# Two expert layers on one Trainium2 core: the result rows of each expert are scattered to their token's place by rank of the choice, and summed from plain loads

## The chip, the cores and the metric

The kernel runs on one core of one Trainium2 chip. The metric is the device time of one execution in microseconds (us). Engines are named as in the profile: PE (TensorE matmuls), PEld (its weight loads), DVE (VectorE), ACT (ScalarE), POOL (GpSimd) and SP (SyncE, which here only issues transfers). "ACTq", "SPq" and "POOLq" are an engine's own queue of such issuing instructions.

## The reference

Two layers of a diffusion backbone over 512 tokens of width 1,024. Each layer ends in a mixture of 16 experts. The router picks one group of four experts for a token and two experts inside it:

```python
def moe_route(flat, router_w, router_b):
    s = jax.nn.sigmoid((flat @ router_w).astype(jnp.float32))
    biased = s + router_b.astype(jnp.float32)
    grp_score = jnp.sum(lax.top_k(biased.reshape(n, 4, 4), 2)[0], axis=-1)
    g_sel = jnp.argmax(grp_score, axis=-1)
    in_group = (jnp.arange(16) // 4)[None, :] == g_sel[:, None]
    _, idx = lax.top_k(jnp.where(in_group, biased, -jnp.inf), 2)
    w = jnp.take_along_axis(s, idx, axis=-1)
    w = w / jnp.sum(w, axis=-1, keepdims=True)

for e in range(16):
    hid = jax.nn.silu(flat @ w_gate[e]) * (flat @ w_up[e])      # 1024 -> 512
    out = out + combine[:, e:e + 1] * (hid @ w_down[e])         # 512 -> 1024
```

So 512 tokens give 1,024 result rows of 4 KB, 64 to an expert on average. What a token receives is the weighted sum of two such rows.

## The kernel before

The kernel is written engine by engine, with semaphores counted. The two layers' expert parts (`moe(0, block)` and `moe(1, block)`) differ only in their data and in what follows them.

**Lists.** At the start of an expert part DVE turns the scores into the two chosen experts of each token and their places in the experts' lists. PE multiplies one-hot matrices of the places with the token numbers (L2106) and so writes, for each expert, a list of up to 128 token numbers. An expert with fewer tokens has empty places, which hold token 0. Were an expert chosen by more than 128 tokens, a second, slow branch (`If(most > P)`) would take the rest; in the traced execution no engine enters it.

**Steps.** One step handles one expert, and the order inside it is written by hand. POOL fetches the expert's 128 rows with one indirect DMA from `xh_scratch` (`fetch`, L1827) four steps ahead. PE transposes them (L2113). All matmuls are made of high and low parts: ACT casts each weight half to its high part (`high`, L1855), DVE subtracts it from the weights to get the low part (`low`, L2011), and PE multiplies 24 times 512 columns for gate, up and down each (L2130, L2145). SP loads the weights in halves of 1 MB into three ring slots. DVE multiplies the result by a gate into `y_sb` (`rows_out`, L2035; two halves at L2077 for the last expert). PE's step e waits with its last third for `rows_out` of expert e-1. `y_sb` has two buffers: `rows_out(e)` waits for the store of expert e-2.

**Stores.** ACT stores the 128 rows of an expert to the expert's own 128 rows of `y_scratch` (`store`).

**Tail.** After the last store has landed (`moe_stored`), POOL fetches with eight indirect DMAs (4 tiles of 128 tokens, 2 choices each; `Combine.fetch`, L2379) each token's two result rows by the row numbers `row_of`. DVE adds each to the residual `x` with its weight (`Combine.add`, L2394). Behind it:

- in layer 0: squares, norm and pooling of layer 1's mixer on ACT, POOL and PE, weights multiplied by a gate on DVE (`p_wg`, L2486 and L2488), the loads of the next router's rows on SP (`front1.load_rows`, L258 to L260, which overwrite the raw pooling weights and so wait for `p_wg`), and `front1.scales` (L324), which stands on DVE ahead of its part of the pooled columns (L2497);
- in layer 1: the final norm (L2574 on ACT, L221 and L223 on POOL, L2591 on DVE) and the stores of the output.

`rows_out` with its two waits:

```python
def rows_out(n, u, down_used, stored):
    dve.wait_ge(s_used, down_used)
    dve.wait_ge(s_yst[u], stored)
    V.tensor_tensor(y_sb[:, u, :], bank[:, 6:8, :], gate2_b[:], ALU.mult).then_inc(s_y, 1)
```

Of the kernel before, what the change touches and what calls it, by code (L numbers as in the profile page):

```python
# [49 lines left out]
LIST_N = NE * SEQ  # L50
# [15 lines left out]
def constants():  # L66
# [34 lines left out]
    token = np.arange(SEQ, dtype=np.int32).reshape(NT, P).T  # L101
# [9 lines left out]
def build_program(nc, a, out):  # L111
    ctx = ExitStack()
    with ctx, nc.allow_non_contiguous_dma(reason="short rows of small tables"):
# [21 lines left out]
        list_dram = nc.dram_tensor("list_scratch", [SEQ // P - 1, P, NE], I32).ap()  # L135
        y_dram = nc.dram_tensor("y_scratch", [LIST_N, D], F32).ap()
# [29 lines left out]
        row_of = sb("row_of", [P, 2, NT], U32)  # L166
# [1517 lines left out]
        def moe(l, block):  # L1684
# [50 lines left out]
            listed, at_small[0] = carve(at_small[0], 2 * NT * NE // 2)  # L1735
# [3 lines left out]
            row_tmp = small_tile("row_tmp", [P, 2, 2, NT])  # L1739
# [3 lines left out]
            lists_more = small_tile("lists_more", [P, SEQ // P - 1, NE], I32)  # L1743
            idx = small_tile("idx", [P, 1], U32)
# [17 lines left out]
            s_yst = [e_(f"y_stored{u}") for u in range(2)]  # L1762
# [7 lines left out]
            FIRST_BANK, LIST_BANK = 4, 3  # L1770
# [54 lines left out]
            def _(pool):  # L1825
                def fetch(u, rows):
                    pool.indirect_dma_start(out=xg[:, u, :], out_offset=None, in_=xh_dram,  # L1827
                                            in_offset=bass.IndirectOffsetOnAxis(ap=rows, axis=0)
                                            ).then_inc(s_xg[u], 16)
# [4 lines left out]
                fetch(0, idx[:])  # L1834
                nc.gpsimd.memset(mark[:], 0.0).then_inc(s_first_rows, 1)  # L1835
                pool.wait_ge(s_lists, 1)
                for m in range(1, NE):
                    u = m % 2
                    if m >= 2:
                        pool.wait_ge(s_gt, m - 1)  # L1840
                        pool.wait_ge(s_xg[u], 16 * (m // 2))
                    fetch(u, lists[:, m:m + 1])
# [4 lines left out]
            def _(act):  # L1847
# [25 lines left out]
                def store(e, u):  # L1873
                    act.wait_ge(s_y, e + 1)
                    act.dma_start(y_dram[bass.ds(e * P, P), :], y_sb[:, u, :]).then_inc(s_yst[u], 16)

                def step(e, u):
# [15 lines left out]
                    if not (isinstance(e, int) and e == 0):  # L1893
                        store(e - 1, 1 - u)
# [14 lines left out]
                store(LAST - 1, 0)  # L1909
                for hf in range(2):  # L1910
                    act.wait_ge(s_y, LAST + 1 + hf)
                    cols_ = slice(hf * HALF, (hf + 1) * HALF)
                    act.dma_start(y_dram[LAST * P:NE * P, cols_], y_sb[:, 1, cols_]).then_inc(s_yst[1], 16)
                for u in range(2):
# [700 lines left out]
```

## Time and profile before

| | us |
|---|---|
| median of 3 runs | 1114.15 (1113.95 to 1116.16) |
| the profiled execution's own time | 1112.38 |
| its span, first to last instruction | 1110.7 |
| busy: PE, DVE, ACT, POOL | 989.0, 939.0, 626.4, 104.4 |
| expert part of layer 0, up to its last result rows | 418.9 to 720.6 |
| tail of layer 0 and layer 1's mixer and router | 720.6 to 778.1 |
| expert part of layer 1, up to its last result rows | 778.1 to 1080.2 |
| tail of layer 1 | 1080.2 to 1110.7 |

The busy times are sums over the whole span; the span less an engine's busy time is its idle time. The last four lines come from the timeline. The traffic of the whole execution was 332.41 MB at a mean of 299 GB/s.

### The profile page before, as it was taken

To read this page: it belongs to the slowest core of one execution; us is meant where nothing else is said; L and a number is where in the kernel's file an instruction comes from. 1 tells how busy PE (TensorE), PEld (TensorE's weight loads), DVE (VectorE), ACT (ScalarE), POOL (GpSimd) and SP (SyncE) were. 2 spreads that over 40 slices of the span, in tenths; PEclk is the share of its full clock that TensorE was granted. 3 is DMA by queue.
4 is the path that set the end of the run, shared out by engine and by line. 5 is a ranking of instruction groups with operands and counts; after the bars stand their busy time and mean duration, and the time that the engine had idled before them with its cause. 6 is when DMAs were issued, how large, how long until landed. Compare 5 with 4: busy or idle time off the path is not lost. (4 is left out here: it accounts for less than half of the span.)

```text
span 1110.7 us, 14060 instructions
## 1 busy us (share of the span) xinstructions
PE 989.0 (89%) x4898; PEld 802.4 (72%) x4898; DVE 939.0 (85%) x1045; ACT 626.4 (56%) x770; POOL 104.4 (9%) x132
## 2 busy tenths in 40 slices
PE   6689999999798986999999999948799999999980
PEld 1467877777676865788888888737578888888870
DVE  5768988998797858899999999865899999999975
ACT  1635233324676135777777777443477777777741
POOL 0200120000110002000000000042300000000005
PEclk9989999999999998999999999969799999999995
DMA  9726878942301836999999999876599999999946
GB/s 368 286 75 211 280 244 308 323 172 96 151 1 53 309 113 237 345 413 414 415 413 415 413 414 412 296 259 263 205 353 413 413 415 413 414 413 414 414 169 236
DMA packets 148263, 332.41 MB, mean 299 GB/s; under 512 B 16444, under 2 KB 18404, under 8 KB 148088
## 3 DMA queue, kind: packets, MB, share of 16 engines
q1 hardware_dynamic: 127592, 278.72, 65.5%
q10 hardware_dynamic: 13712, 27.92, 7.2%
q0 software_dynamic: 6912, 25.17, 6.0%
q8 instruction: 27, 0.44, 0.2%
q14 instruction: 20, 0.16, 0.0%
HBM read 308.67 MB, written 23.11 MB: 299 GB/s over the span
## 5 line engine op out<-in xcount | busy, mean ns | idle before, releaser
L1855 ACT CAST w_hi<-ring 128x2048 fp32r<-128x2048 f32 x192 | 367.1, 1916 | 112.2 <-PE bank L2130 55.1
L2011 DVE TENSOR_TENSOR w_lo<-ring,w_hi 128x2048 fp32r<-128x2048 f32 x192 | 428.8, 2284 | 1.4 <-POOL mark L1835 1.0
L2130 PE MATMUL bank<-w_hi,xT_hi 128*128 128x512 f32 x512 | 203.4, 397 | 5.2 <-DVE xT_lo L2018 5.2
L2130 PE MATMUL bank<-w_hi,xT_lo 128*128 128x512 f32 x512 | 200.0, 391 | 0.0
L2130 PE MATMUL bank<-w_lo,xT_hi 128*128 128x512 f32 x512 | 199.5, 390 | 0.0
L1511 PE MATMUL bank<-ring_last_parts,arena_parts 128*128 128x512 f32 (+1 forms) x320 | 117.5, 398 | 8.0 <-DVE x_parts L1073 6.5
L2130 PEld LDWEIGHTS bank<-w_hi,xT_hi 128*128 128x128 f32 x512 | 96.1, 188 | 26.1 <-DVE xT_lo L2018 6.9
L2130 PEld LDWEIGHTS bank<-w_hi,xT_lo 128*128 128x128 f32 x512 | 96.2, 188 | 20.8
L2130 PEld LDWEIGHTS bank<-w_lo,xT_hi 128*128 128x128 f32 x512 | 96.3, 188 | 19.1
L1511 PE MATMUL bank<-ring_parts,arena_parts 128*128 128x512 f32 (+1 forms) x256 | 101.0, 395 | 0.0
L1145 DVE SCALAR_TENSOR_TENSOR gate_b<-ring,silu_c,gate_b 128x512 f32<-128x512 f32 x126 | 95.5, 758 | 4.5
L2145 PE MATMUL bank<-w_hi,hT_hi 128*128 128x512 f32 x240 | 93.6, 390 | 0.0
L2145 PE MATMUL bank<-w_lo,hT_hi 128*128 128x512 f32 x240 | 93.5, 389 | 0.0
L2145 PE MATMUL bank<-w_hi,hT_lo 128*128 128x512 f32 x240 | 93.4, 389 | 0.0
L1827 POOL DMA_INDIRECT shared<-xh_scratch,shared x32 | 37.5, 1171 | 428.1 <-PE bank L2113 406.3
L1511 PE MATMUL bank<-ring_last_parts,x_parts 128*128 128x512 f32 x192 | 77.7, 405 | 0.0
L1511 PEld LDWEIGHTS bank<-ring_last_parts,arena_parts 128*128 128x128 f32 x320 | 61.1, 194 | 20.9 <-DVE x_parts L1073 5.8
L1511 PEld LDWEIGHTS bank<-ring_parts,arena_parts 128*128 128x128 f32 x256 | 49.4, 193 | 8.8
L2145 PEld LDWEIGHTS bank<-w_hi,hT_hi 128*128 128x128 f32 x240 | 45.1, 188 | 9.3
L2145 PEld LDWEIGHTS bank<-w_hi,hT_lo 128*128 128x128 f32 x240 | 45.0, 188 | 9.4
L2145 PEld LDWEIGHTS bank<-w_lo,hT_hi 128*128 128x128 f32 x240 | 45.1, 188 | 9.3
L869 ACT ACTIVATE ada_junk<-bank 128x128 f32<-128x128 f32 x80 | 21.0, 278 | 48.0 <-PE bank L1481 25.2
(273 smaller groups left out, 1427.8 us busy)
## 6 DMA issues: line engine op xcount, KB each, us to landing
ring<-in_moe_w_gate SPq DMA_DIRECT2D x64, 1024.0 KB, 9.1
ring<-in_moe_w_down SPq DMA_DIRECT2D x64, 1024.0 KB, 9.6
ring<-in_moe_w_up SPq DMA_DIRECT2D x64, 1024.0 KB, 11.8
ring<-in_ada_w SPq DMA_DIRECT2D x18, 2048.0 KB, 9.1
y_scratch<-shared ACTq DMA_DIRECT2D x30, 512.0 KB, 6.2
ring<-in_w_in ACTq DMA_DIRECT2D x21, 512.0 KB, 4.6
shared<-in_ada_w SPq DMA_DIRECT2D x6, 1024.0 KB, 13.3
x_res<-in_x SPq DMA_DIRECT2D x8, 512.0 KB, 12.1
```

The lines of the kernel that those rows point to most:

```text
L869: last = nc.scalar.activation(ada_junk[:, c * P:(c + 1) * P], bank[:, 7 if i < IN_PROJ else 6 + i - IN_PROJ, c * P:(c + 1) * P], ACT.Ident ...
L1145: ins = nc.vector.scalar_tensor_tensor(ada_acc[:, i % 2, :], w[:, k, :], silu_c[:, 0, k:k + 1], onto, ALU.mult, ALU.add)
L1511: last = pe.matmul(acc(u)[:, c0:c1], hs[h_], ws[w_], start=(kk == 0 and i == 0), stop=(kk == KD - 1 and i == 2))
L1827: pool.indirect_dma_start(out=xg[:, u, :], out_offset=None, in_=xh_dram, in_offset=bass.IndirectOffsetOnAxis(ap=rows, axis=0)).then_inc(s_ ...
L1855: nc.scalar.copy(w_hi[:, buf(u, p), :], half(raw(e, p))).then_inc(s_hi, 3 if isinstance(e, int) and (e, p) == (-1, 3) else 1)
L2011: V.tensor_tensor(w_lo[:, buf(u, p), :], half(raw(e, p)), w_hi[:, buf(u, p), :].bitcast(F32), ALU.subtract).then_inc(s_lo, 3 if isinstance ...
L2130: last = pe.matmul(bank[:, b, :], xs[:, kk, :], ws[:, k, :], start=(kk == 0 and i == 0), stop=(kk == KD - 1 and i == 2))
L2145: last = pe.matmul(bank[:, 6 + hf, :], xs[:, kk, :], ws[:, k, at], start=(kk == 0 and i == 0), stop=(kk == KE - 1 and i == 2))
```

## The change

- Each list entry gets a second number, the destination: the token's number, plus 512 if this expert is the token's choice with the higher expert number ("rank 1"). `y_scratch` shrinks to 2 x 512 rows: rank 0 of all tokens, then rank 1. Eight more matmuls on PE make the destination lists (`dests`), DVE gets a few small operations for them.
- Lists hold the number minus 1,024, and 1,024 is added as they are copied, so that an empty place holds 1,024. The fetches get a bounds check and skip such places; the stale row in `xg` is multiplied and its result is dropped.
- ACT's plain stores go. POOL scatters `y_sb` by an indirect DMA with a bounds check (`scatter`), each behind a fetch in POOL's program.
- The weights of a token's two choices are put in order of rank.
- The tail's eight indirect fetches go. SP issues eight plain loads of 512 KB into ring slots 2 and 1 (`Combine.load`): four of rank 0 once all experts but the last are scattered, four of rank 1 once the last is. DVE adds all of rank 0 first. In layer 0 the gated pooling weights are made in two parts between the adds, and `front1.load_rows` waits for both; in layer 1 the load of the final norm's weights moves behind the eight loads.

```diff
-            def fetch(self, pool, most, moe_stored):
-                def tiles(written):
-                    for t in range(NT):
-                        for c in range(2):
-                            pool.indirect_dma_start(
-                                out=self.rows[:, c, t, :], out_offset=None, in_=y_dram[0:written, :],
-                                in_offset=bass.IndirectOffsetOnAxis(ap=row_of[:, c, t:t + 1], axis=0)
-                            ).then_inc(self.loaded[c][t], 16)
...
+            def load(self, sp, y_scattered):
+                for c in range(2):
+                    y_scattered(sp, NE - 1 + c)
                     for t in range(NT):
+                        at = (c * NT + t) * P
+                        sp.dma_start(self.rows[c][:, t, :], y_dram[at:at + P, :]).then_inc(self.loaded[c][t], 16)
...
+            def y_scattered(eng, experts):
+                for u in range(2):
+                    eng.wait_ge(s_yst[u], 16 * ((experts + 1 - u) // 2))
...
                 def fetch(u, rows):
                     pool.indirect_dma_start(out=xg[:, u, :], out_offset=None, in_=xh_dram,
-                                            in_offset=bass.IndirectOffsetOnAxis(ap=rows, axis=0)
+                                            in_offset=bass.IndirectOffsetOnAxis(ap=rows, axis=0),
+                                            bounds_check=SEQ - 1, oob_is_err=False
                                             ).then_inc(s_xg[u], 16)
...
+                def scatter(e):
+                    pool.wait_ge(s_y, NE + 1 if e == LAST else e + 1)
+                    if e == 0:
+                        pool.wait_ge(s_dests, 1)
+                    pool.indirect_dma_start(out=y_dram,
+                                            out_offset=bass.IndirectOffsetOnAxis(ap=dests[:, e:e + 1], axis=0),
+                                            in_=y_sb[:, e % 2, :], in_offset=None, bounds_check=2 * SEQ - 1,
+                                            oob_is_err=False).then_inc(s_yst[e % 2], 16)
+
-                for m in range(1, NE):
+                for m in range(1, NE + 5):
                     u = m % 2
+                    if m < NE:
                         if m >= 2:
                             pool.wait_ge(s_gt, m - 1)
                             pool.wait_ge(s_xg[u], 16 * (m // 2))
                         fetch(u, lists[:, m:m + 1])
+                    if m >= 5:
+                        scatter(m - 5)
...
-                def store(e, u):
-                    act.wait_ge(s_y, e + 1)
-                    act.dma_start(y_dram[bass.ds(e * P, P), :], y_sb[:, u, :]).then_inc(s_yst[u], 16)
...
+                    for c in range(2):
+                        ins = V.tensor_tensor(later[:, c], e_sel[:, c], e_sel[:, 1 - c], ALU.is_gt)
+                    link(ins)
+                    link(V.scalar_tensor_tensor(dest[:], later[:], float(SEQ),
+                                                token_f[:].unsqueeze(1).to_broadcast([P, 2, NT]), ALU.mult, ALU.add))
+                    for c in range(2):
+                        ins = V.tensor_tensor(listed[:, c, :, NE:2 * NE], pick[:, c], cols(dest[:, c], NE), ALU.mult)
+                    ins.then_inc(s_dest, 1)
...
                 rows_T(1, 16)
+                pe.wait_ge(s_dest, 1)
+                for c in range(2):
+                    for t in range(NT):
+                        last = pe.matmul(bank[:, DEST_BANK, DEST_AT:DEST_AT + NE], slot_of[:, c, t, :],
+                                         listed[:, c, t, NE:2 * NE], start=(c == 0 and t == 0), stop=(c == 1 and t == NT - 1))
+                last.then_inc(s_in_dests, 1)
                 product(3, -1, 0, 2, 0)
...
@@ layer 0, SP and DVE behind the expert part
-                sp.wait_ge(p_wg, 1)
+                combine.load(sp, y_scattered)
+                sp.wait_ge(p_wg, 2)
                 sp.wait_ge(combine.done, NT - 1)
                 front1.load_rows(sp)
...
+                for t in range(NT):
+                    combine.add(dve, 0, t)
                 dve.wait_ge(tables, 16 * 8)
...
+                gated_weights(0)
                 for t in range(NT):
-                    combine.add(dve, t)
+                    combine.add(dve, 1, t)
+                gated_weights(1)
                 front1.scales(dve)
...
@@ layer 1, SP and DVE behind the expert part
                 y_ready(sp)
+                combine.load(sp, y_scattered)
                 sp.dma_start(fin_w, a["final_norm_w"].partition_broadcast(P)).then_inc(f_ld, 16)
...
-                combine.add(dve, 0)
-                combine.add(dve, 1)
+                for t in range(NT):
+                    combine.add(dve, 0, t)
+                combine.add(dve, 1, 0)
+                combine.add(dve, 1, 1)
                 dve.wait_ge(f_ld, 16)
                 for t in range(NT):
                     if t + 2 < NT:
-                        combine.add(dve, t + 2)
+                        combine.add(dve, 1, t + 2)
                     dve.wait_ge(f_rs, t + 1)
```

How POOL's program reads at the start of an expert part, before (a row is a line, an operation and its tiles; `shared` holds `xg` and `y_sb`):

```order
L1831 CAST shared<-shared 128x128
L1832 MEMSET shared 128x128
L1827 DMA shared<-xh_scratch,shared 128x1024
L1835 MEMSET mark 1x1
L1827 DMA shared<-xh_scratch,shared 128x1024 x15
L1844 TENSOR_LOAD max_count
```

And after the change, the same place:

```order
L1837 CAST shared<-shared 128x128
L1838 MEMSET shared 128x128
L1832 DMA shared<-xh_scratch,shared 128x1024
L1841 MEMSET mark 1x1
L1832 DMA shared<-xh_scratch,shared 128x1024 x5
L1849 DMA y_scratch<-shared 1024x1024
L1832 DMA shared<-xh_scratch,shared 128x1024
L1849 DMA y_scratch<-shared 1024x1024
```

From the sixth fetch on, each is followed by the scatter of the expert five places earlier; after the last fetch the scatters of experts 11 to 15 stand in a row, ahead of the load of `max_count`.

DVE's program behind layer 0's expert part, before:

```order
L2484 SCALAR_TENSOR_TENSOR mod<-mod 128x8
L2485 TENSOR_SCALAR mod<-mod 128x8
L2486 TENSOR_TENSOR gate_b<-gate_b,shared 128x1024
L2488 TENSOR_TENSOR arena<-shared,gate_b 128x4x256 x2
L2394 SCALAR_TENSOR_TENSOR x_res<-arena,weight,x_res 128x1024 x8
L324 SCALAR_TENSOR_TENSOR shared<-shared,arena 128x1024
L2497 TENSOR_SCALAR arena<-bank,mod 128x512 x4
```

And after:

```order
L2428 SCALAR_TENSOR_TENSOR x_res<-ring,weight,x_res 128x1024 x4
L2517 SCALAR_TENSOR_TENSOR mod<-mod 128x8
L2518 TENSOR_SCALAR mod<-mod 128x8
L2519 TENSOR_TENSOR gate_b<-gate_b,shared 128x1024
L2521 TENSOR_TENSOR arena<-shared,gate_b 128x4x256
L2428 SCALAR_TENSOR_TENSOR x_res<-ring,weight,x_res 128x1024 x4
L2521 TENSOR_TENSOR arena<-shared,gate_b 128x4x256
L323 SCALAR_TENSOR_TENSOR shared<-shared,arena 128x1024
L2533 TENSOR_SCALAR arena<-bank,mod 128x512 x4
```

The gate and half of the gated weights have moved from before the adds to between the two ranks' adds, the other half behind them.

SP's program at the end of layer 1, before:

```order
L2228 REGISTER_ALU
L2228 COMPARE_AND_BRANCH
L2243 UNCONDITIONAL_BRANCH
L2564 DMA shared<-in_final_norm_w 128x1024
L2567 DMA out<-shared 128x1024 x4
L2548 UNCONDITIONAL_BRANCH
```

And after:

```order
L2255 COMPARE_AND_BRANCH
L2270 UNCONDITIONAL_BRANCH
L2420 DMA ring<-y_scratch 128x1024 x8
L2600 DMA shared<-in_final_norm_w 128x1024
L2603 DMA out<-shared 128x1024 x4
L2584 UNCONDITIONAL_BRANCH
```

The eight loads now stand ahead of the final norm's weights in SP's queue.

## Rows read from the trace of the kernel before

**Rows 1.** The profile page, its first line.

```profile
span 1110.7 us, 14060 instructions
```

**Rows 2.** Busy times in one step: PE, PEld, DVE, ACT, POOL; clock, DMA share, GB/s.

```profile
857.70:875.40 17.70, 17.70 (x86) 14.78 (x85) 16.78 (x11) 13.31 (x10) 0.94 (x1) 1.00 1.04 414
```

**Rows 3.** Waits from 850 to 1040 us: total, times, longest; DVE's only row.

```profile
DVE hT_lo L2028 <- ACT hT_hi L1871: 10.2, 11, 0.9
```

**Rows 4.** Timeline, POOL and DVE in two steps: start, us, what, [idle before].

```profile
851.52 0.94 POOL L1827 DMA_INDIRECT shared<-xh_scratch,shared  x1 [16.75 <-PE bank L2113]
869.20 0.94 POOL L1827 DMA_INDIRECT shared<-xh_scratch,shared  x1 [16.75 <-PE bank L2113]
869.32 6.68 DVE L2011 TENSOR_TENSOR w_lo<-ring,w_hi 128x2048 fp32r<-128x2048 f32 x3
```

**Rows 5.** Timeline, POOL's indirect DMAs that start inside a DVE instruction.

```profile
790.36 2.28 DVE L2011 TENSOR_TENSOR w_lo<-ring,w_hi 128x2048 fp32r<-128x2048 f32 x1
790.71 2.74 POOL L1827 DMA_INDIRECT shared<-xh_scratch,shared  x1 [2.68 <-DVE shared L2054]
...
1091.98 2.60 DVE L2394 SCALAR_TENSOR_TENSOR x_res<-shared,weight,x_res 128x1024 f32<-128x1024 f32 x2 [1.23 <-DMA shared<-y_scratch,row_of]
1093.10 0.97 POOL L2379 DMA_INDIRECT shared<-y_scratch,row_of  x1 [0.30 <-issue]
```

**Rows 6.** Heads of the expert parts: timeline, and one piece of the chain (786.70).

```profile
431.62 1.09 PE L2113 MATMUL bank<-ident,shared 128*128 128x128 f32 x8 [0.57 <-DMA shared<-xh_scratch,shared]
...
786.70 4.24 DMA shared<-xh_scratch,shared
...
787.68 0.38 PE L2106 MATMUL bank<-shared 128*128 128x16 f16 x8 [1.64 <-DVE shared L1980]
787.91 2.91 PE L2084 MATMUL bank<-w_hi 128*128 128x512 f32 x6
...
807.45 1.23 DVE L2018 TENSOR_TENSOR xT_lo<-bank,xT_hi 128x1024 fp32r<-128x1024 f32 x1 [3.17 <-PE bank L2130]
```

**Rows 7.** Layer 1's tail: timeline and pieces of the chain (1080.24, 1090.26).

```profile
1074.72 1.22 DVE L2035 TENSOR_TENSOR shared<-bank,gate_b 128x1024 f32<-128x1024 f32 x1
1080.24 4.09 DMA y_scratch<-shared
1090.26 6.30 DMA shared<-y_scratch,row_of
1100.53 2.60 DVE L2394 SCALAR_TENSOR_TENSOR x_res<-shared,weight,x_res 128x1024 f32<-128x1024 f32 x2
```

**Rows 8.** Landing times: the eight indirect fetches of layer 1's tail.

```profile
L2379 POOL DMA_INDIRECT shared<-y_scratch,row_of x8: 933/937/1302, 1085.3 to 1094.4; - x8
...
DMA to landing us min/median/max: 4.1/6.0/6.3
```

**Rows 9.** Landing time of the final norm's weights, 512 KB, alone in flight.

```profile
DMA to landing us min/median/max: 3.9/3.9/3.9
```

**Rows 10.** Layer 0's tail, timeline.

```profile
719.90 0.69 DVE L2077 TENSOR_TENSOR shared<-bank,gate_b 128x512 f32<-128x512 f32 x1 [1.96 <-PE bank L2185]
721.30 1.22 DVE L2486 TENSOR_TENSOR gate_b<-gate_b,shared 128x1024 f32<-128x1024 f32 x1
722.55 2.36 DVE L2488 TENSOR_TENSOR arena<-shared,gate_b 128x1024 f32<-128x1024 f32 x2
737.34 3.93 DVE L2394 SCALAR_TENSOR_TENSOR x_res<-arena,weight,x_res 128x1024 f32<-128x1024 f32 x3 [0.26 <-DMA arena<-y_scratch,row_of]
739.10 0.43 SPq L259 DMA_DIRECT2D arena<-in_norm_ffn_w  x1
742.35 2.18 ACT L2445 ACTIVATE arena<-x_res,rstd 128x1024 f32<-128x1024 f32 x2
744.28 1.23 DVE L324 SCALAR_TENSOR_TENSOR shared<-shared,arena 128x1024 f32<-128x1024 f32 x1 [3.01 <-DMA arena<-in_norm_ffn_w]
746.36 2.97 DVE L2497 TENSOR_SCALAR arena<-bank,mod 128x512 f32<-128x512 f32 x4 [0.85 <-PE bank L2515]
```

More of the change, by code:

```diff
@@ L49 @@
 SLOT_W = 4096
-LIST_N = NE * SEQ
+NO_ROW = 2 * SEQ
 SH1, SC1, G1, SH2, SC2, G2 = range(6)
@@ L1761, in moe @@
             most = []
-            s_yst = [e_(f"y_stored{u}") for u in range(2)]
+            s_yst = [e_(f"y_scattered{u}") for u in range(2)]
+            s_dest, s_in_dests, s_dests = e_("destinations"), e_("destinations_multiplied"), e_("destination_lists_ready")
             s_dc = e_("dve_chain")
             LAST = NE - 1
-            FIRST_BANK, LIST_BANK = 4, 3
+            FIRST_BANK, LIST_BANK, DEST_BANK = 4, 3, 5
+            DEST_AT = 2 * NT * NE
             def last_step(e):
@@ L1908, in _ @@
                 hid_high(LAST, hT_last_hi)
[L1909 to L1914, printed above, removed]
-                    act.wait_ge(s_yst[u], 16 * (NE // 2 + 1 + u))
             @block.vector
@@ L2003, in weights_of_tokens @@
                     link(V.tensor_tensor(weight[:], weight[:], w_sum[:].unsqueeze(1).to_broadcast([P, 2, NT]), ALU.mult))
-                for u in range(2):
-                    V.memset(idx_zero[:, u:u + 1], 0.0).then_inc(s_yst[u], 16)
+                    for h in range(2):
+                        for c in range(2):
+                            ins = V.tensor_tensor(w_pair[:, h, c], weight[:, c], later[:, c if h else 1 - c], ALU.mult)
+                    link(ins)
+                    V.tensor_tensor(weight[:], w_pair[:, :, 0], w_pair[:, :, 1], ALU.add)
+                V.memset(idx_zero[:], 0.0)
                 def low(e, u, p):
@@ L2044, in step @@
                     low(e, u, 3)
-                    if stored is not None:
+                    if not (isinstance(e, int) and e == 0):
                         rows_out(e - 1, 1 - u, 6 * (e + 1), stored)
@@ L2053, in _ @@
                 dve.wait_ge(s_in_lists, 1)
-                V.tensor_copy(lists[:], bank[:, LIST_BANK, 0:NE]).then_inc(s_lists, 1)
+                V.tensor_scalar(lists[:], bank[:, LIST_BANK, 0:NE], float(NO_ROW), None, ALU.add).then_inc(s_lists, 1)
                 low(-1, 0, 1)
@@ L2361, in y_ready, with __init__ @@
                 eng.wait_ge(s_y, NE + 1)
-            return most[0], moe_stored, y_ready, s_pool
+            def y_scattered(eng, experts):
+                for u in range(2):
+                    eng.wait_ge(s_yst[u], 16 * ((experts + 1 - u) // 2))
+            return y_scattered, y_ready, s_pool
         class Combine:
-            def __init__(self, name, rows):
-                self.rows = rows
+            def __init__(self, name):
+                self.rows = [ring[:, s, :].rearrange("p (t c) -> p t c", t=NT) for s in (2, 1)]
                 self.loaded = [[sem(f"{name}_rows{c}_{t}") for t in range(NT)] for c in range(2)]
@@ L2472, in _ @@
             def _(pool):
-                combine.fetch(pool, most, moe_stored)
                 for t in range(NT):
@@ L2577, in _ @@
             def _(pool):
-                combine.fetch(pool, most, moe_stored)
                 for t in range(NT):
```

146 lines of the change are left out of this document (76 added, 70 removed).

## The prediction

> **What bounds the kernel now.** I start from the span [rows 1] and ask of each of the four stretches in the table above which wait ends last. In the steps of an expert part the answer is PE: in one step of 17.70 us it is busy for 17.70 us at full clock [rows 2], two successive fetches lie 17.68 us apart [rows 4], and no row of the waits in that stretch has PE waiting. Next to it stands DVE with 16.78 us of work; what is left to it is one gap of 0.93 us per step [rows 2, 3], in which it waits for ACT and so for PE. So whatever the change saves in a step (transfer bytes, ACT's issue of the store) saves nothing, and only what takes DVE more than 0.92 us a step would show. The time to be had lies outside the steps: in the two tails, where PE stands still while stores land, POOL issues fetches and DVE adds [rows 7, 10], and in the two heads, where lists and first rows are made [rows 6].
>
> **The steps: no cost, with one cover to name.** Per step one scatter is added on POOL. POOL's program puts it behind the fetch, and its input has long been written by then, so it is issued at the fetch's start + 0.94 + 0.30 us, that is at 870.44, in the middle of DVE's three splits of the weights [rows 4]. Nothing shows a scatter, but rows 5 show an indirect DMA there. The fetch at 790.71 starts inside a split that ends at 792.64 and itself ends at 793.45, 0.81 us later: POOL waits for the end of the DVE instruction. The one at 1093.10 starts inside the first of two adds that follow each other; it gets in at their boundary (1093.28) and ends 0.79 us behind it, and the two adds take 2.60 us, as two do elsewhere [rows 5, 7]. So POOL loses up to 2.3 us, which nobody waits for (the next fetch comes 17 us later, `y_sb` is wanted two steps later), and DVE loses less than 0.1 us, which its 0.93 us cover. If that cover were gone, each microsecond of DVE would lengthen 28 steps (experts 0 to 13, two layers). The Trainium skill ("SBUF — State Buffer", Who interferes with whom) says of a DVE instruction with two SBUF inputs and a POOL instruction that reads SBUF that the second to start is blocked for the whole of the first. By that rule POOL's wait agrees with the trace, but DVE would lose 0.94 us behind the boundary; the trace's undelayed second add speaks against it, and it is rival 4.
>
> **The heads: +0.7 and -0.3 us.** Eight matmuls for the destinations stand between the rows' transposes and the up product, on PE's path. The eight for the lists took 0.38 us [rows 6]; so +0.35 us a layer, +0.7 in all. Their input is ready: the new DVE operations take the place of those for `row_of`, about 0.1 to 0.2 us each, and the five more behind them (0.6 us) fall into 3.17 us of idle DVE [rows 6]. The first fetch skips its empty places. It took 4.24 us to land; PE waited 0.57 us for it in layer 0, while in layer 1 PE's filler matmuls last until 790.82 and the rows landed at 790.94 [rows 6]. Fewer rows can therefore save at most 0.57 + 0.12 us; I take 0.3. What the bounds check costs no row shows. From below it is nothing; from above I let POOL's instruction double, +0.9 us in each head and for each scatter in a tail. I take nothing, since the instruction walks the same 128 indices.
>
> **Layer 1's tail: -4.1 us.** Expert 14's rows are in `y_sb` at 1075.94, expert 15's at 1080.22 [rows 7]. A scatter's landing: a plain store of 256 KB took 4.09 us here [rows 7], indirect fetches of 512 KB 4.1 to 6.3 [rows 8]; I take 4.4 with about half the rows valid, bounds 4.1 and 6.3. So the scatter of 14 lands at 1080.4 and SP issues rank 0 from 1080.45. A load of 512 KB alone lands after 3.9 us [rows 9]: 1084.35. Further ones follow at the rate of the steps' plain loads, 414 GB/s [rows 2], 1.27 us each. The scatter of 15, beside them, lands at about 1085.2 and costs them 0.6 us. That is before rank 0's last load (1088.8), so rank 1's four loads are queued without a gap: 1090.0 to 1093.8, and the final norm's weights, now last in the queue, at 1095.1. DVE adds at 1.30 us each [rows 7]: rank 0 by 1090.1, two tiles of rank 1 by 1092.7. Then it waits for the norm's weights, which is the new wait of this tail: the third add ends at 1096.4, the first normed tile (1.28 us) at 1097.7, the last add at 1099.0. Before it ended at 1103.13 [rows 7], and 7.57 us lay behind it to the end of the span [rows 1], the same operations as after. The gain is 4.1 us. The bounds: without the wait for the norm's weights the last add ends at 1097.1, a gain of 6.0. If the loads come as the fetches did (the first at 1089.4, the fifth at 1096.56 [rows 7, 8], 1.79 us each), the norm's weights land at 1099.3, the last add ends at 1103.2, and nothing is gained.
>
> **Layer 0's tail: -0.2 us.** The same adds are done earlier, but not what waits for them. Expert 15's rows are ready at 720.6 [rows 10], expert 14's 4.3 us before, as in layer 1; scatter landed 720.7, rank 0 landed 724.7 to 729.1, added by 730.4. Now the gate and half of the gated weights stand between the ranks, 1.22 + 1.18 us and two tiny operations [rows 10], which before lay in DVE's idle time: 733.0. Four adds: 738.2, against 741.27 before [rows 10], 3.1 us earlier. But behind them come 1.18 us of gated weights, and only then does SP load the next router's rows: the norm's row is issued at about 739.8, where before it was at 739.10 [rows 10], before the last add. It landed 5.15 us after its issue, with other loads; alone one takes 3.9 [rows 9]. I take 4.9, so 744.7; the scale on DVE ends at 745.95, and the pooled columns, which before began at 746.36 after waiting 0.85 us for PE [rows 10], begin there: 0.4 us earlier. ACT is in the way too: its eight passes over the tiles at 1.1 us [rows 10] begin with the first finished tile at 734.3 and end at 743.6 to 744.4, against 744.53. I take 0.2 us. The bounds: -2 (loads land at once) and +1.7 (a scatter landing in 6.3 us shifts all of it by 1.9).
>
> **The sum.** -4.1 - 0.2 + 0.7 - 0.3 = -3.9 us. Against the profiled execution's own 1112.38 that is 1108.5. The median of the runs lies 1.8 us above it, at 1114.15, so I predict 1110.3.
>
> **The rivals.**
> 1. The loads do not limit: the norm's weights land before DVE wants them and the scatters land in 4.1 us or less. Layer 1 gains 6.0, layer 0 up to 2, the heads cost 0.4: 1106.5. For it speaks that the chip is otherwise silent in these stretches; against it, that nine loads and a scatter, 5 MB, need 11.4 us at 414 GB/s from an issue that cannot come before 1080.2.
> 2. The tails give nothing back: the transfers come at the fetches' spacing of 1.79 us, or each scatter lands in 6.3 us, which shifts layer 0 by +1.7 and layer 1's stream by 1.9. Gains of 0 to 1 in layer 1 against +0.7 in the heads: 1113.5 to 1115. The fetches' rows speak for it; that POOL issued those one by one every 1.24 us speaks against it.
> 3. DVE becomes the bound. A scatter that holds DVE for d us costs 28 x (d - 0.92). It decides from d = 1.06, where it eats the 3.9 us; a scatter that held DVE for 1.5 us would give 1110.3 + 16 = 1126. Against it stand the adds of rows 5.
> 4. POOL's instruction blocks DVE for its whole 0.94 us: 28 x 0.02 = 0.6 us less gain, 1110.9. This is the rule cited above.
> 5. The bounds check makes indirect DMAs dearer: +0.9 in each head, +0.9 for the scatters of each tail, 3.6 together: 1113.9, and above 1116.4 only from three times the instruction's time.
>
> **How the numbers follow.** My forecast (a gain of 2.3 to 5.5 us) has 0.42, rival 1 0.15, rival 2 0.24, rival 3 0.08, rival 4 0.04, rival 5 0.07. A measurement of this kernel can tell 0.2%, 2.2 us, from no change. Faster by more: the forecast, rivals 1 and 4 and a little of 2, 0.62. The same: most of rivals 2 and 5, 0.27. Slower: rival 3 and the rest, 0.11. The range reaches from rival 1's side, 1107.0, to 1114.2 within rivals 2 and 5. The forecast's own range is 1108.6 to 1111.9.
>
> **What the profile after would show.** Steps still 17.68 us apart, DVE's splits still 2.28 us, and scatters of up to 3.1 us on POOL beside them. Eight new matmuls of 0.38 us per head. In layer 1 a wait of DVE for the norm's weights of 2 to 3 us and a last add that ends 18.8 us after expert 15's rows are ready (22.9 before), with the same 7.6 us behind it; no wait for rank 0 between its adds above 0.1 us. In layer 0 the scale of the router's rows waits for its load, and the pooled columns begin without waiting for PE. The traffic falls by about 17 MB. I am wrong if a step is longer than 17.7 us, if a scatter takes more than 6.3 us to land in a tail, or if the eight loads land more than 1.5 us apart.

## The result, and the profile after

The changed kernel takes 1125.9 us (median of 4 runs, 1124.2 to 1127.2) against 1115.1 us (4 runs, 1114.0 to 1116.2) for the kernel before on the same chip: ratio 1.0096, 95% interval 1.0077 to 1.0116. It is 1% slower, where I had forecast 0.35% faster. The profiled execution of after took 1125.31 us for a span of 1123.5. All ratios are of undisturbed executions: one of the ten of kernel e5 below took 4774 us and is left out.

Where the time went is first a question of stages. I cut each trace at four marks: the issue of `gate2_b`'s load in each layer (start of an expert part) and the end of the last half of `y_sb` (its end).

| us | span | front | experts 0 | tail 0 | experts 1 | tail 1 |
|---|---|---|---|---|---|---|
| before | 1110.7 | 418.9 | 301.7 | 57.5 | 302.1 | 30.5 |
| after | 1123.5 | 426.6 | 302.2 | 61.3 | 302.6 | 30.7 |

The largest piece, 7.7 us, lies in the front, all of whose instructions are the same in both programs. That row decides what to look for: something that the diff changes without changing an instruction. The windows of both traces show it. First the kernel before, windows (us, busy time and count of PE, PEld, DVE, ACT, POOL; clock, DMA share, GB/s):

```profile
10.00:20.00 10.00, 10.00 (x19) 1.75 (x18) 9.79 (x15) 0.00 (x0) 0.00 (x0) 1.00 1.05 409
450.00:700.00 250.00, 250.00 (x1188) 208.74 (x1187) 238.17 (x142) 186.14 (x128) 11.23 (x12) 1.00 1.03 407
```

Then the same windows of the kernel after, and the step window of [rows 2] again:

```profile
10.00:20.00 10.00, 9.90 (x21) 1.75 (x20) 9.76 (x14) 0.00 (x0) 0.00 (x0) 1.00 1.05 387
450.00:700.00 250.00, 248.61 (x1187) 206.85 (x1184) 232.91 (x140) 185.25 (x126) 59.72 (x26) 1.00 1.01 373
...
857.70:875.40 17.70, 17.70 (x86) 14.80 (x85) 16.79 (x11) 13.29 (x10) 4.68 (x2) 1.00 1.04 378
```

In the stretch from 10 to 20 us both programs stream the same plain loads with full DMA engines (share 1.05), and after moves 387 GB/s where before moved 409. This row is the evidence. In the steps a lower rate was to be expected, since skipped rows are not moved (315.66 MB in all, 332.41 before), and the two effects are mixed there: e1 below, which skips the same rows and has the old addresses, also shows a DMA share of 1.01 from 450 to 700 us, at 378 GB/s. The steps themselves held: PE 17.70 of 17.70 us, DVE 16.79 against 16.78 [rows 2].

POOL in two steps of after, and DVE's splits beside the first pair, timeline (start, us, what, [idle before]):

```profile
863.98 6.68 DVE L2028 TENSOR_TENSOR w_lo<-ring,w_hi 128x2048 fp32r<-128x2048 f32 x3
864.35 2.80 POOL L1832 DMA_INDIRECT shared<-xh_scratch,shared  x1 [12.69 <-PE bank L2134]
867.46 1.88 POOL L1849 DMA_INDIRECT y_scratch<-shared  x1 [0.31 <-issue]
882.03 2.80 POOL L1832 DMA_INDIRECT shared<-xh_scratch,shared  x1 [12.70 <-PE bank L2134]
885.14 1.89 POOL L1849 DMA_INDIRECT y_scratch<-shared  x1 [0.31 <-issue]
```

Steps are still 17.68 us apart, and POOL is held up beside DVE's splits, now at the fetch too (0.94 us in [rows 4]). The three splits, with a fetch and a scatter beside them, take the 6.68 us that they took before [rows 4].

Layer 1's tail in after, timeline:

```profile
1089.58 0.97 POOL L1849 DMA_INDIRECT y_scratch<-shared  x1 [8.86 <-DVE shared L2053]
1092.85 10.87 SPq L2420 DMA_DIRECT2D ring<-y_scratch  x8
1093.60 0.97 POOL L1849 DMA_INDIRECT y_scratch<-shared  x1 [3.05 <-DVE shared L2098]
1096.64 2.57 DVE L2428 SCALAR_TENSOR_TENSOR x_res<-ring,weight,x_res 128x1024 f32<-128x1024 f32 x2 [3.81 <-DMA ring<-y_scratch]
1100.96 1.28 DVE L2428 SCALAR_TENSOR_TENSOR x_res<-ring,weight,x_res 128x1024 f32<-128x1024 f32 x1 [1.76 <-DMA ring<-y_scratch]
1102.59 1.28 DVE L2428 SCALAR_TENSOR_TENSOR x_res<-ring,weight,x_res 128x1024 f32<-128x1024 f32 x1 [0.34 <-DMA ring<-y_scratch]
...
1105.74 2.54 DVE L2428 SCALAR_TENSOR_TENSOR x_res<-ring,weight,x_res 128x1024 f32<-128x1024 f32 x2 [1.86 <-DMA ring<-y_scratch]
...
1111.92 1.28 DVE L2428 SCALAR_TENSOR_TENSOR x_res<-ring,weight,x_res 128x1024 f32<-128x1024 f32 x1 [3.63 <-DMA shared<-in_final_norm_w]
```

and the chain that ended last through it (start, us, what):

```profile
1092.89 0.50 issue
1093.39 0.21 POOLq L1864
1093.60 8.30 DMA y_scratch<-shared
...
1103.76 8.13 DMA shared<-in_final_norm_w
```

Expert 15's rows are written at 1092.82. SP issues rank 0's four loads from 1092.85 on, 0.39 to 0.48 us apart; POOL's scatter starts 0.75 us after the first of them, with two issued ahead of it (1092.85 and 1093.24) and two just behind (1093.72 and 1094.19). It lands after 8.30 us, where I had 4.4 to 5 us. Rank 1's loads therefore start at 1101.98 and the norm's weights, last in the queue, land at 1111.89. The last add (in no row here) runs from 1114.31 to 1115.59: 22.8 us behind the last rows, as in before (22.9).

### The profile page after: what moved, and what is told of

It is laid out like the page before. It is cut to its first block and busy times, and to the rows that moved or that the text cites. A ratio compares the mean times of both kernels' runs of the same rounds, so it can differ in the third digit from the quotient of the medians.

```text
span 1123.5 us, 14056 instructions
## 1 busy us (share of the span) xinstructions
PE 997.2 (89%) x4914; PEld 807.3 (72%) x4914; DVE 939.9 (84%) x1055; ACT 625.6 (56%) x770; POOL 191.3 (17%) x148
## 2 busy tenths in 40 slices
DMA packets 147976, 315.66 MB, mean 281 GB/s; under 512 B 20508, under 2 KB 22468, under 8 KB 147800
## 5 line engine op out<-in xcount | busy, mean ns | idle before, releaser
L1832 POOL DMA_INDIRECT shared<-xh_scratch,shared x32 | 75.1, 2348 | 346.2 <-PE bank L2134 296.7
L1510 PE MATMUL bank<-ring_last_parts,arena_parts 128*128 128x512 f32 (+1 forms) x320 | 120.3, 407 | 3.8 <-DVE x_parts L1072 2.4
L2151 PEld LDWEIGHTS bank<-w_lo,xT_hi 128*128 128x128 f32 x512 | 96.3, 188 | 18.9
L1849 POOL DMA_INDIRECT y_scratch<-shared x32 | 66.5, 2077 | 119.4 <-DVE shared L2053 106.7
## 6 DMA issues: line engine op xcount, KB each, us to landing
x_res<-in_x SPq DMA_DIRECT2D x8, 512.0 KB, 12.6
```

The lines of the kernel that those rows point to most:

```text
L1510: last = pe.matmul(acc(u)[:, c0:c1], hs[h_], ws[w_], start=(kk == 0 and i == 0), stop=(kk == KD - 1 and i == 2))
L1849: pool.indirect_dma_start(out=y_dram, out_offset=bass.IndirectOffsetOnAxis(ap=dests[:, e:e + 1], axis=0), in_=y_sb[:, e % 2, :], in_offset ...
L2151: last = pe.matmul(bank[:, b, :], xs[:, kk, :], ws[:, k, :], start=(kk == 0 and i == 0), stop=(kk == KD - 1 and i == 2))
```

## The experiments

What the diff changes without an instruction is an address. Tiles are laid out one behind the other in each partition's memory, and `row_of` (32 bytes a partition), which the change removes, stands ahead of `ring`, the slots of the weights. In the compiled program `ring` starts at byte 42,752 of a partition before, 167 x 256, and at 42,720 after; `shared` stands 49,152 bytes (192 x 256) behind it and shifts with it. The first four kernels put this on trial. In all kernels below `filler` is a tile that nothing uses.

**e1.** The changed kernel with the 32 bytes put back; e2 and e3 the kernel before with 32 and, by `[P, 4, NT]`, 64 bytes of filler at the same place.

```diff
+        filler = sb("filler", [P, 2, NT], U32)
         max_count = sb("max_count", [P, 1], I32)
```

> The changed kernel with one unused tile of 32 bytes a partition where row_of stood, so that every tile allocated behind it (max_count, the weight ring, shared and all stage tiles) lies where it lay before the change; nothing reads or writes the filler. Theory A (addresses): the change took 32 bytes out of the SBUF layout, and loads into tiles that start 32 bytes off a multiple of 64 move fewer bytes a second; then the first fetch's list is ready at 426 to 427 us after the start as before (434.4 in the changed kernel), the first 50 us move 409 GB/s at their best (388 in the changed kernel), and the time falls by about 8 us in the front and up to 2 more in the tails, to 1115 to 1118. Rival B (the lost time is work: another program, other code, longer instruction streams): no difference to the changed kernel, 1125 to 1127.

> The kernel before with an unused tile of 32 bytes a partition ahead of max_count, so that the ring and all later tiles lie 32 bytes further, at the same remainder of 64 as in the changed kernel. Theory A: the front takes 7 to 8 us longer, and the time is 1122 to 1127 with no other part of the change in it. Rival B: 1115, as before.

> The kernel before with an unused tile of 64 bytes there: everything is moved, but the remainder of 64 stays. Theory A: no difference to the kernel before (1114 to 1116). A rival to A in which any move of the tiles, or a new program, costs time: 1122 or more, like the run with 32 bytes.

**e4.** The kernel before with empty places skipped by bounds-checked fetches, everything else as it was (lists hold 1,024 for an empty place).

```diff
-                                            in_offset=bass.IndirectOffsetOnAxis(ap=rows, axis=0)
+                                            in_offset=bass.IndirectOffsetOnAxis(ap=rows, axis=0),
+                                            bounds_check=SEQ - 1, oob_is_err=False
```

> The kernel before with one part of the change: empty places of the lists hold 1,024 and the fetches carry the bounds check that skips them; stores, tails and addresses as before. My prediction: heads 0.3 us shorter, nothing else, 1114.8. Rival: the bounds-checked fetch starts about 0.8 us later behind its release and runs into DVE's splits (2.8 us on POOL instead of 0.94), which costs the heads up to 0.8 us each on the path, +1 to +2 us, and nothing in the steps.

Measured, with what the later ones gave (GB/s in the windows 10 to 20 and 450 to 700 us; a ratio is always to the kernel before on the same chip):

| kernel | ring at | ratio, 95% interval | GB/s | front | experts 0 | tail 0 | experts 1 | tail 1 |
|---|---|---|---|---|---|---|---|---|
| e1 | 42,752 = 167 x 256 | 1.0028 (1.0013 to 1.0043) | 409, 378 | 423.4 | 301.8 | 59.6 | 302.0 | 29.5 |
| e2 | 42,784 | 1.0116 (1.0086 to 1.0147) | 387, 393 | 426.8 | 305.5 | 59.4 | 304.9 | 31.1 |
| e3 | 42,816 | 1.0101 (1.0078 to 1.0123) | 387, 394 | 423.2 | 304.9 | 57.8 | 307.6 | 31.0 |
| e4 | 42,752 | 0.9994 (0.9981 to 1.0006) | 408, 393 | 424.9 | 301.0 | 59.1 | 301.6 | 30.3 |
| e5 | 42,240 = 165 x 256 | 1.0009 (0.9993 to 1.0024) | 409, 405 | 421.0 | 302.1 | 58.1 | 302.5 | 30.3 |
| e6 | 42,880 = 335 x 128 | 1.0072 (1.0047 to 1.0098) | 387, 392 | 421.3 | 306.7 | 60.0 | 305.8 | 30.8 |
| e7 | 42,752 | 0.9989 (0.9971 to 1.0007) | 408, 379 | 421.7 | 302.6 | 57.9 | 302.1 | 27.5 |
| e8 | 42,752 | 1.0017 (1.0000 to 1.0033) | 409, 376 | 423.5 | 302.6 | 60.8 | 302.0 | 29.9 |
| e9 | 42,752 | 0.9983 (0.9970 to 0.9996) | 409, 379 | 419.0 | 302.6 | 58.2 | 302.5 | 28.0 |
| e10 | 42,752 (shared +32) | 1.0020 (1.0007 to 1.0033) | 393, 405 | 419.6 | 302.3 | 58.6 | 302.3 | 30.7 |
| e11 | 42,752 | 1.0010 (0.9998 to 1.0021) | 409, 379 | 420.9 | 302.6 | 60.6 | 301.7 | 29.3 |
| e12 | 42,752 | 0.9980 (0.9968 to 0.9992) | 409, 407 | 419.0 | 302.0 | 58.1 | 302.4 | 28.6 |

The kernels that skip empty places (e1, e4, e7, e8, e9, e11) move fewer bytes, so their second rate is not to be compared with the others'. What follows from the first four: 32 unused bytes make the kernel before 1.2% slower, and 32 bytes make most of the changed kernel's loss go away. They did not do all that theory A said of e1: the front came back by 3.2 us and not by 8, and the median was 1120.2 us, not 1115 to 1118 (before took 1117.4 on this chip, 2.3 us more than where the forecasts started). e3 brought down the first form of my theory, a multiple of 64: with 64 bytes of filler the rate is 387 GB/s too. What e1's ring and before's have in common, and e2's, e3's and after's lack, is a start on a multiple of 256 (and of 128, which e6 separates). e4 shows the skipping harmless, and what it costs and gives: chain pieces of the first fetch of layer 1 in e4,

```profile
793.48 0.75 issue
794.23 3.61 DMA shared<-xh_scratch,shared
```

where in before POOL needed 0.27 us from the release and the rows 4.24 [rows 6]: a start 0.5 us later, a landing 0.6 us sooner.

In the steps e2 shows where the lower rate goes. Its waits from 450 to 700 us (total, times, longest):

```profile
ACT w_hi L1856 <- DMA ring<-in_moe_w_gate: 19.4, 10, 2.4
ACT w_hi L1856 <- DMA ring<-in_moe_w_up: 18.9, 22, 2.1
```

In before the same list has one wait for a load in the ring, of 0.6 us. A step moved 7.3 MB in 17.7 us at 414 GB/s [rows 2]; at 387 it would need 18.9 us, and at the 398 that the same window of e2 shows 18.4, both estimates. The kernel before stood just at the edge of its loads, and 5% of rate turn it from PE-bound to load-bound in part of the steps: an expert part takes 3 to 6 us longer in e2, e3 and e6. After moves about 0.5 MB less a step (16.75 MB over 32 experts), and its expert parts took 302.2 and 302.6 us; that the saved bytes pay for the lower rate fits this, but no run separates the two.

**e5, e6: which multiple.** e5 declares `ident`, 512 bytes, behind `shared` instead of ahead of the ring; e6 is the kernel before with 128 bytes of filler.

```diff
-        ident = sb("ident", [P, P])
...
         shared = sb("shared", [P, SHARED_W])
+        ident = sb("ident", [P, P])
```

> The kernel before with one 512-byte tile (ident) declared behind shared: the ring moves down by 512 bytes, from 42,752 (167 x 256) to 42,240 (165 x 256), and the rest is the same program. Theory A (what counts is whether the ring and shared start on a multiple of 256 bytes): no change, ratio 0.998 to 1.002, and 405 to 412 GB/s in the window 10 to 20 us. Theory B (any other address than that of the kernel before costs, or a rule finer or coarser than 256 bytes, such as one of 512): 385 to 395 GB/s there and a ratio of 1.01.

> The kernel before with an unused tile of 128 bytes ahead of the ring: 42,880, a multiple of 128 and not of 256. Theory A (256 bytes): as with 32 and 64 bytes of filler, 385 to 395 GB/s in the window 10 to 20 us and a ratio of 1.010 to 1.012. Theory B (a multiple of 128 is enough): 405 to 412 GB/s and a ratio of 1.00.

The same two windows of e6:

```profile
10.00:20.00 10.00, 10.00 (x19) 1.78 (x18) 9.79 (x15) 0.00 (x0) 0.00 (x0) 1.00 1.05 387
...
450.00:700.00 250.00, 246.59 (x1163) 203.44 (x1162) 233.18 (x139) 183.47 (x125) 14.26 (x12) 1.00 1.03 392
```

Theory A both times by the rate: another address that is a multiple of 256 costs nothing, and at one of 128 alone the loads are as slow as with 32 bytes of filler. The ratio of e6, 1.0072, is smaller than the 1.010 to 1.012 that I expected. The rate of 387 GB/s is the same 224, 32, 64 and 128 bytes past a multiple of 256 (after, e2, e3, e6). The Trainium skill ("DMA: Bandwidth & Descriptors", How a descriptor splits into AXI transactions) says, of what a descriptor reads, that transactions of at most 256 bytes start at multiples of 256, so that an unaligned piece takes one more. These loads differ in where they write. If the rule held for writes as well, a row of 2 KB would take 9 transactions for 8 and one of 4 KB 17 for 16, an estimate of 6 to 12% by that page; the traces show 409 to 387, 5.4%. The multiple of 256 agrees with these runs; that transactions are the reason was not measured here.

**e10: which tile.** The 32 bytes between `ring` and `shared`.

```diff
         ring = sb("ring", [P, 3, SLOT_W])
+        filler = sb("filler", [P, 2, NT], U32)
         shared_parts = parts_of("shared_parts", SHARED_W)
```

> The kernel before with the unused 32 bytes declared behind the ring: the ring stays at 42,752 (a multiple of 256), shared moves to 91,936 (not one). Theory A (it is the weights' destination that counts, and the experts' weights land in the ring): 405 to 409 GB/s in the steps (450 to 700 us), the expert parts at 301.5 to 302.5 us, ratio 0.999 to 1.003. Theory B (shared, which holds the fetched rows and the rows that are stored, counts as much): expert parts of 304.5 us or more, 392 GB/s there, ratio 1.007 to 1.012.

In the first 20 us, when loads go to both tiles in turn, the rate is 393; in the steps, when the weights go to the ring, it is 405 and the expert parts are at most 0.6 us longer; in all 0.2%. So it is the destination of the large loads that counts.

**e7, e8: the tails, with the ring aligned.** e7 is e1 with the norm's weights ahead of the row loads in layer 1, and in layer 0 all gated weights ahead of the adds, as before the change. e8 holds all row loads until the last scatter landed.

```diff
-                for t in range(NT):
-                    combine.add(dve, 0, t)
                 dve.wait_ge(tables, 16 * 8)
...
                 gated_weights(0)
-                for t in range(NT):
-                    combine.add(dve, 1, t)
                 gated_weights(1)
+                for c in range(2):
+                    for t in range(NT):
+                        combine.add(dve, c, t)
...
+                sp.dma_start(fin_w, a["final_norm_w"].partition_broadcast(P)).then_inc(f_ld, 16)
                 combine.load(sp, y_scattered)
-                sp.dma_start(fin_w, a["final_norm_w"].partition_broadcast(P)).then_inc(f_ld, 16)
```

and in e8 besides

```diff
-                    y_scattered(sp, NE - 1 + c)
+                    y_scattered(sp, NE)
```

> The changed kernel with the ring put back on a multiple of 256 bytes (filler of 32), the load of the final norm's weights issued ahead of the eight row loads of layer 1, and in layer 0's tail both halves of the gated weights ahead of all the adds, as before the change. Theory A (what is left of e1's loss stands in DVE's wait for the final norm's weights and in the adds behind the gated weights): against e1 layer 1's tail gives back 2.0 to 2.8 us (29.5 to about 27), layer 0's 1 to 2.5 us (59.6 to 57 to 58.5), in all a ratio of 0.998 to 1.000. Theory B (the tails end with the rows' landing whatever their order): no more than 1 us, ratio 1.002 to 1.003.

> e7 with one wait changed: in both tails the loads of the rows of rank 0 wait for the last scatter too, so that it lands with no load in flight. Theory A (the last scatter took 8.3 us in the changed kernel because 2 MB of rank-0 loads stood ahead of it): it lands in 4.1 to 4.8 us from its issue, and all eight loads land in 10.5 us or less after that; either tail is within 1.5 us of e7's. Theory B (the landing is slow by itself, for the bounds check or the rows' own writes): it still takes over 6 us, and both tails are 3 us or more longer than e7's.

e7 gives back 2.0 us in layer 1's tail and 1.7 in layer 0's against e1, and the ratio falls to 0.9989. Theory A. In e8 the chain through layer 1's tail reads

```profile
1089.68 4.39 DMA y_scratch<-shared
...
1095.01 5.46 DMA ring<-y_scratch
```

where e7's has

```profile
1084.93 8.72 DMA y_scratch<-shared
1094.09 4.50 DMA ring<-y_scratch
```

so the scatter with the row loads held back lands in 4.39 us: it is neither the bounds check nor the rows' own writing that made it 8.3. But it was not alone. The load of the norm's weights, 512 KB, was issued just ahead of it (e8, timeline):

```profile
1088.93 0.34 SPq L2599 DMA_DIRECT2D shared<-in_final_norm_w  x1
1089.68 0.97 POOL L1850 DMA_INDIRECT y_scratch<-shared  x1 [3.30 <-DVE shared L2099]
```

With no row load and no load of the norm's weights beside it a scatter landed sooner still: expert 15's in layer 0 of e8 in 3.5 us, expert 14's in layer 1 in 3.2 to 3.4 us (after, e7, e8, e9 and e11; 4.0 in e1). My theory A held for the landing, and missed for the tails: they are 2.4 and 2.9 us longer than e7's, not within 1.5. The four loads that waited had used time in which the scatter leaves the DMA engines idle: from 1089.7 to 1094.1 they are busy for a share of 0.53 in e8, and for 0.82 while e9's scatter is under way.

**e9, e11, e12: how far it goes.** e9 is e7 with the final norm's weights in `gate1_b`, idle in layer 1, loaded before SP waits for the last rows. e12 is the same edit in the kernel before. e11 is e9 with the third and fourth rank-0 load held until the last scatter landed.

```diff
-            fin_w, at = carve(0, D)
-            fin, at = carve(at, NT, D)
+            fin_w = gate1_b[:]
+            fin, at = carve(0, NT, D)
...
-                y_ready(sp)
                 sp.dma_start(fin_w, a["final_norm_w"].partition_broadcast(P)).then_inc(f_ld, 16)
+                y_ready(sp)
```

and in e11 besides, in the loop over the loads,

```diff
+                        if c == 0 and t == NT // 2:
+                            y_scattered(sp, NE)
```

> e7 with the final norm's weights kept in gate1_b, which layer 1 doesn't use, and their load issued before SP waits for the last y, so that they land under the last expert. Theory A (in e7 the 0.5 MB of norm weights stand ahead of the row loads: the first add began 6.3 us after the last y, in e1 4.4 us): the first add begins 4.2 to 5 us after the last y and layer 1's tail ends 1 to 1.9 us sooner than e7's 27.5, so 25.6 to 26.5 us, ratio 0.996 to 0.998. Theory B (the eight adds and four norms of DVE, or the last scatter, end the tail): within 0.5 us of e7's tail, ratio 0.999.

> e9 with the rank-0 loads of the third and fourth tile held until the last scatter landed, so that it has 1 MB of loads ahead of it and not 2. Theory A (each MB ahead delays the scatter by 2 to 2.5 us, and the last rows of rank 1 set the end): the scatter lands 5.5 to 6.5 us from its issue, the first add of rank 1 begins 1 to 2 us sooner than in e9, layer 1's tail within 1 us of e9's. Theory B (as in e8, what is held is lost whole, since the scatter alone can't keep the DMA engines busy): both tails 1 to 2 us longer than e9's.

> The kernel before with the final norm's weights kept in gate1_b and loaded under the last expert. In its trace DVE waits 3.9 us for these weights in layer 1's tail. Theory A (that wait is on the path): the tail gets 1.5 to 3 us shorter than 30.5, ratio 0.997 to 0.9985. Theory B (the sixth to eighth fetch of rows land hardly sooner than the weights, so that the wait only moves to them): tail of 30 us or more, ratio 0.9995 to 1.0005.

In e9 the first add begins 3.7 us after the last rows (e7: 6.3), but the tail is 28.0 us, no shorter than e7's: theory B. Its DVE in the tail, timeline:

```profile
1086.08 2.66 DVE L2429 SCALAR_TENSOR_TENSOR x_res<-ring,weight,x_res 128x1024 f32<-128x1024 f32 x2 [3.68 <-DMA ring<-y_scratch]
1090.88 2.50 DVE L2429 SCALAR_TENSOR_TENSOR x_res<-ring,weight,x_res 128x1024 f32<-128x1024 f32 x2 [2.14 <-DMA ring<-y_scratch]
1095.04 2.48 DVE L2429 SCALAR_TENSOR_TENSOR x_res<-ring,weight,x_res 128x1024 f32<-128x1024 f32 x2 [1.66 <-DMA ring<-y_scratch]
...
1098.81 1.28 DVE L2429 SCALAR_TENSOR_TENSOR x_res<-ring,weight,x_res 128x1024 f32<-128x1024 f32 x1 [1.28 <-DMA ring<-y_scratch]
```

With the norm's weights out of the way DVE waits for rows instead, and the scatter's landing (8.09 us) sets when those of rank 1 come. e11's scatter lands in 6.17 us, within theory A's 5.5 to 6.5. SP's loads beside the two scatters, e9 and then e11, timeline:

```profile
1082.43 10.65 SPq L2421 DMA_DIRECT2D ring<-y_scratch  x8
1083.18 0.98 POOL L1850 DMA_INDIRECT y_scratch<-shared  x1 [3.29 <-DVE shared L2099]
...
1085.74 10.00 SPq L2423 DMA_DIRECT2D ring<-y_scratch  x8
1086.48 0.98 POOL L1850 DMA_INDIRECT y_scratch<-shared  x1 [3.29 <-DVE shared L2099]
```

In both the first two loads are issued ahead of the scatter (in e9 at 1082.43 and 1082.83). What e11 takes away are the two that e9 issues 0.12 and 0.59 us behind its start (1083.30 and 1083.77), and they cost the scatter 1.9 us: it is delayed by loads issued ahead of it and by loads issued right behind it. By the plain loads around it, the landing takes 3.2 to 4.1 us with none, 4.39 with 0.5 MB (e8), 6.17 and 4.5 with 1 MB (e11, layers 1 and 0) and 7.4 to 8.7 with 2 MB (both layers of after, e1 and e9): it grows with them, but these are too few for a price per MB. e11's tails are 2.4 and 1.3 us longer than e9's all the same (theory B there). e12 took 1.9 us off the tail of the kernel before, theory A.

e9 at 0.9983 and e12 at 0.9980 both beat the kernel before by a little, and not each other: brought back to a multiple of 256 and with its tails ordered well, the change is worth about nothing over the kernel before with the one edit.

## Why the prediction was wrong, point by point

- **What it left out.** The step that failed first is the one that was not there: I took stretches with identical instructions as costing nothing, "The steps: no cost" and the front not named at all. The removal of `row_of` moved the destination of all large loads off a multiple of 256. With everything else equal, after against e1, that is 1.0096 against 1.0028, 0.7% or about 7.6 us (each a ratio to before on its own chip); the difference of their profiled spans is 7.2: 3.2 in the front, 1.0 in the expert parts, 1.7 and 1.2 in the tails. None of my rivals had this, and the time fell outside the range by 11.7 us.
- **Layer 1's tail, -4.1.** With the ring aligned it gave -1.0 (29.5 against 30.5). The step "the scatter of 15, beside them, lands at about 1085.2 and costs them 0.6 us", and with it "rank 1's four loads are queued without a gap", failed: the scatter took 7.94 us in e1, not 4.4, since it shares the time with rank 0's loads. These were mis-sized too, "1.27 us each". DVE in e1's tail, timeline:

```profile
1091.20 1.28 DVE L2429 SCALAR_TENSOR_TENSOR x_res<-ring,weight,x_res 128x1024 f32<-128x1024 f32 x1 [4.41 <-DMA ring<-y_scratch]
1093.21 1.28 DVE L2429 SCALAR_TENSOR_TENSOR x_res<-ring,weight,x_res 128x1024 f32<-128x1024 f32 x1 [0.73 <-DMA ring<-y_scratch]
1095.71 2.48 DVE L2429 SCALAR_TENSOR_TENSOR x_res<-ring,weight,x_res 128x1024 f32<-128x1024 f32 x2 [1.21 <-DMA ring<-y_scratch]
1099.38 2.51 DVE L2429 SCALAR_TENSOR_TENSOR x_res<-ring,weight,x_res 128x1024 f32<-128x1024 f32 x2 [1.20 <-DMA ring<-y_scratch]
1104.69 1.28 DVE L2429 SCALAR_TENSOR_TENSOR x_res<-ring,weight,x_res 128x1024 f32<-128x1024 f32 x1 [2.80 <-DMA shared<-in_final_norm_w]
```

  Expert 15's rows were ready at 1086.80. The first load came as forecast (4.4 us behind them, 4.1 said), the next two 2.0 and 2.5 us apart, rank 1's first 12.6 us behind (9.8 said), the norm's weights 17.9 us behind (14.9 said). The wait for these weights was there (2.80 us in e1, 3.63 in after; 2 to 3 said). Three signs that I had named for being wrong were met: DVE waited between rank 0's adds, loads landed more than 1.5 us apart, and the scatter took more than 6.3 us. Rival 2 was right here in size and largely in cause, loads about as far apart as the fetches or further and a late scatter, though only the last scatter was late (expert 14's took 3.2 to 4.0 us).
- **Layer 0's tail, -0.2.** e1 took 59.6 where kernels with before's tail and an aligned ring took 57.5, 58.1, 58.1 and 59.1: +0.5 to +2.1, around the bound of +1.7 that I gave for a late scatter, rather than the value. The path was the one I had named, through the norm's row of the next router. DVE in e1, then in e7, where all gated weights stand ahead of the adds:

```profile
751.68 1.23 DVE L324 SCALAR_TENSOR_TENSOR shared<-shared,arena 128x1024 f32<-128x1024 f32 x1 [6.67 <-DMA arena<-in_norm_ffn_w]
753.05 2.97 DVE L2534 TENSOR_SCALAR arena<-bank,mod 128x512 f32<-128x512 f32 x4
...
750.32 2.97 DVE L2533 TENSOR_SCALAR arena<-bank,mod 128x512 f32<-128x512 f32 x4 [2.99 <-PE bank L2551]
```

  In e1 that row was issued 20.2 us behind expert 15's rows (19.2 said) and landed 6.3 us later (4.9 said), and the pooled columns began right behind its scale, 27.9 us behind the rows where before had 25.8. In e7 they begin at 26.1 and wait for PE again. So half of the gated weights behind the rank-1 adds did cost, about 1.8 us.
- **The heads, +0.7 and -0.3.** Both smaller: the eight new matmuls took 0.18 us on layer 1's chain (I had 0.35), and the first fetch saved nothing. It needed 0.77 + 3.88 us from its release, 0.27 + 4.24 before [rows 6]. The bounds check, which I had taken at nothing, costs a start 0.5 us later, and skipped rows give back 0.4 to 0.6 us of the landing (e4).
- **The steps.** Right by every row I named: 17.68 us apart, DVE unhurt, scatters of 1.9 us beside the splits. Rival 3 and the blocking of rival 4 are out: three splits take 6.68 us with a fetch and a scatter inside them, as in before, and in e1 the expert parts took 301.8 and 302.0 us with 32 scatters more. Rival 5 is out as a loss of time (e4, 0.9994), though a bounds check has a price.
- **The sum.** e1 measured +0.28% (+3.1 us), where my sum was -3.9: 7 us off even with the address mended. The tails account for 4 to 5 of them. The rest is not found: the front, the same program in e1 and before, took 423.4 and 418.9 us in the two profiled executions, a difference no larger than that among other aligned kernels (next point).
- **What stays open.** The front took 418.9 to 424.9 us in nine profiled executions with both tiles aligned and 421.3 to 426.8 in four with neither: means 421.4 and 424.5. That the slower loads cost some 3 us there is likely and not settled, since one profile each scatters as much.

## What to carry to other kernels

After any edit of a tile list, look at where the destinations of the large loads start, and keep them on multiples of 256 bytes: a stretch of identical code at another DMA rate is the sign to look for, and a filler tile is the test. When a kernel is close to its load rate, bytes saved in one place may only hide a loss in another. A small transfer that others wait for lands late when large ones are in flight beside it, issued before it or right after it: put its landing into the forecast with that price. Holding the large ones back until it landed cost more than it saved here (e8, e11), as the DMA engines stood partly idle.

## What was unexpected of the hardware

- The rate of plain loads depends on the start of their destination in a partition: 409 GB/s on multiples of 256 bytes (42,240 and 42,752), 387 at 42,720, 42,784, 42,816 and 42,880, however far from such a multiple.
- A scatter of a tile landed in 3.2 to 4.1 us with no large load beside it and in 7.4 to 8.7 us with 2 MB of them on SP's queue, though it is on another queue. In layer 1 of e9 half of the 2 MB was issued only after the scatter's start; without that half (e11) it took 6.17 us, not 8.09.
- A bounds-checked indirect DMA started 0.75 us after its release, an unchecked one 0.27 us.
